# Turning the recurrence's gated output on VectorE and GpSimd, with two columns of the output projection interleaved

## The chip, the cores and the metric

The kernel runs on one core of a Trainium2 chip. The metric is the time of one execution in device microseconds (us), as the median of several runs. A core has a matrix engine (TensorE; PE in the profile, its weight loads PEld), VectorE (DVE), ScalarE (ACT), GpSimd (POOL) and SyncE (SP), which issues the weight loads from memory. The engines run their own instruction lists in order and meet at semaphores.

## What is computed

Two transformer-like blocks on one sequence of 256 rows of 2048 numbers: a gated convolution layer, a gated linear recurrence layer (HGRN2), sliding window attention, and a gated feed-forward layer. The change touches the end of the recurrence layer:

```python
def hgrn2_mixer(h, w_in, lb_fwd, lb_bwd, o_norm, w_out):
    u = h @ w_in
    q, a_f, a_b, i, z = jnp.split(u, 5, axis=-1)
    ...
    o = rms_norm(o_fwd + o_bwd, o_norm)
    o = o.transpose(0, 2, 1, 3).reshape(B, S, WIDTH).astype(h.dtype)
    return (o * jax.nn.silu(z)) @ w_out
```

`y = o * silu(z)` is 256 rows by 2048 channels, and the product `y @ w_out` needs it with channels on the partitions, so y must be transposed before the projection.

## The kernel before

Every weight matrix is streamed in chunks of 256 rows by 512 columns (512 KB). A chunk passes four engines: SP loads it into `raw` (four slots), ACT rounds it to `w_hi` (L906), DVE computes the rest `w_lo = raw - w_hi` (L1293), and PE does twelve matmuls with it (L644, L645, L646: high by high, low by high, high by low, for two halves of the contraction and two blocks of rows). ACT may round chunk n only when PE has used chunk n-4. All engines run the same loop over chunks (`stream`), and everything else is hung into this loop by hand: `Hooks().put(i, step)` runs a step on that engine right behind its work on chunk i. So the order of work on an engine is the order of the chunk numbers, and within one number the order of the `put` calls. A step hooked to chunk i of DVE comes before DVE's `w_lo` of chunk i+1, and an engine that waits in a step lets everything behind it wait too.

The stretch at issue is the phase `hgrn_z` (32 chunks, the product that gives z, four column groups of 512) and the phase `hgrn_out` behind it (32 chunks, the output projection, four columns of eight chunks each). Hooks count on from one phase to the next, so chunk 32 is the first of `hgrn_out`. The text numbers chunks this way, from 0 at the start of `hgrn_z` to 63 at the end of `hgrn_out`.

The output of the recurrence comes in four groups of 512 channels. For group k DVE multiplies (`gate(k)`, L1597, into `gate_rows[k]`, that is aftok, abtok, qtok, sz); PE transposes eight 128x128 blocks into the accumulator memory T (`gated_turn(k)`, L595); ACT rounds them to `y_hi` (`hz_hi(k)`, L1181); DVE computes `hy_lo` (`z_lo(k)`, L1298). `GATE_AT = [29, 31, 33, 35]` places PE's four transposes behind chunks 29, 31, 33 and 35; ACT's step is three chunks later and DVE's four (z_lo(0) at 32, z_lo(1) at 35, z_lo(2) at 37, z_lo(3) at 39). The projection takes group k in its chunks 2k and 2k+1 of each column, and PE waits in front of each chunk of the first column until the group is there (`need`, semaphore g_lo).

Group 3's last factor is late: DVE's `o_norm(3)` (L1546, L1548, hook 32) gives sums, GpSimd's `o_power(3)` (L516) raises them to -0.5, DVE's `o_scale(3)` (L1553, L1555, hook 34) waits for that and scales, and `gate(3)` follows at hook 35, behind z_lo(1). GpSimd has nothing else to do in this stretch.

The result of each column is added to x by DVE (`residual`, L1329), two chunks after the column's end. PE has two pairs of accumulators, used in turn by the columns, so column 2 can't begin before column 0's residual. From x, three of the four groups are transposed for the next layer by DVE in blocks of 32x32 (`x_turn`, L1346) and by GpSimd, which moves the blocks between the partition quarters with 16 copies (`x_moves`, L506); the same pair of steps serves the recurrence's inputs (L1581, L522).

Of the kernel before, what the change touches and what calls it, by code (L numbers as in the profile page):

```python
# [30 lines left out]
ACT = mybir.ActivationFunctionType  # L31
# [6 lines left out]
TB = S // P  # L38
# [23 lines left out]
FIRST_LOWS = 2 * CPG  # L62
ACT_TAKES = 4
HB = P // 2
GATE_AT = [29, 31, 33, 35]
TURNED_PARTS = [(2 * c, 2 * c + 2) for c in range(CPG)]
WARM = 14

# [11 lines left out]
class Phase:  # L80
# [6 lines left out]
    def __init__(self, iters, per_iter, chunk0, pair0, uses0, chunks=CPG, columns=4, turns=None):  # L87
        self.chunk0, self.pair0, self.uses0 = chunk0, pair0, uses0
        assert iters == 1 or per_iter % 2 == 0
        self.uses_per = [sum(self.pair(k) == p for k in range(per_iter)) for p in range(2)]  # L90
        self.seq = [(k, c) for k in range(per_iter) for c in range(chunks)]
        if per_iter == 2 * columns:
            self.seq = [(p * columns + k, c) for p in range(2) for ks, cs in (((0, 1), (0, 1)), ((0, 1), (2, 3)), ((2,), range(4)), ((3,), range(4)))
                        for k in ks for c in cs]
        self.seq0 = self.seq
        if turns:
            self.seq0 = [(k, c) for a, b in zip((0, *turns), turns) for k in range(2) for c in range(a, b)] + [kc for kc in self.seq if kc[0] > 1]
        self.last0 = {k: i for i, (k, c) in enumerate(self.seq0) if c == chunks - 1}
        self.last = {k: i for i, (k, c) in enumerate(self.seq) if c == chunks - 1}
        self.chunks, self.in_parts, self.columns = chunks, per_iter == 2 * columns, columns  # L100
        self.chunk1 = chunk0 + iters * len(self.seq)
        self.uses1 = [uses0[p] + iters * self.uses_per[p] for p in range(2)]
# [37 lines left out]
def phases():  # L140
    out, chunk, pair, uses = {}, 0, 0, [0, 0]
    for name, iters, per, more in (
            ("conv_ab", 4, 2, {}), ("conv_z", 1, 4, {}), ("conv_out", 1, 4, {}), ("hgrn", 4, 4, {"turns": (6, 8)}),
            ("hgrn_z", 1, 4, {}), ("hgrn_out", 1, 4, {}), ("kv_q", 1, 5, {}), ("att_out", 1, 8, {"chunks": CPG // 2}),
            ("gate_up", FJ, 2, {"turns": (4, 6, 8)}), ("down", 1, 4, {"chunks": FCH})):
        out[name] = Phase(iters, per, chunk, pair, uses, **more)
        pair = out[name].pair(iters * per)
        chunk, uses = out[name].chunk1, out[name].uses1
    return out
# [23 lines left out]
def build(nc, t, out):  # L173
    ph = phases()
    ctx = ExitStack()
    with ctx:
# [3 lines left out]
        def sem(name):  # L180
            return ctx.enter_context(nc.semaphore(name))
# [106 lines left out]
        def operands(s):  # L288

            b = (s - 1) % 4 if s else 1  # L290
            return (E_more if b >= 2 else E)[:, b % 2, :, :, :]

        def gate_banks(k):
            return T01 if k % 2 else T23

# [17 lines left out]
        g_raw, g_q, g_M, g_act, g_lb, g_D, g_E, g_G, g_mm, g_S = (  # L313
            sem(f"hgrn_{s}") for s in ("raw", "quarters", "moved", "act", "lb", "D", "E", "G", "mm", "S"))
        g_sb, g_K = sem("hgrn_blocks"), sem("hgrn_keys")
        g_av, g_o, g_ss, g_std, g_on, g_zr, g_z, g_y, g_yT, g_hi, g_lo = (
            sem(f"hgrn_{s}") for s in ("av", "o", "ss", "std", "on", "zr", "z", "y", "yT", "yhi", "ylo"))
        a_cs, a_ang, a_ev, a_sq, a_ss, a_std, a_rp, a_T, a_cp = (
# [25 lines left out]
        def by_channel(t):  # L344
            return t.rearrange("p a (b c) -> p (a b) c", c=S)

        x_quarters = (None, 2 * (atok[:, :, :],), 2 * (sm[:, 0:2, :],), (aq[:, :, :], kvtok))
        x_moved = (None, 2 * (by_channel(sq[:, :, :]),), 2 * (by_channel(sm[:, 2:4, :]),), (by_channel(ar), by_channel(asq)))

        def on_tensor(s):  # L350

# [1 line left out]

        def moved_buffers(s):

            return 2 if s == 3 else 1

        def groups_turned(s):

# [19 lines left out]
        def flat(ap):  # L379
            return ap.rearrange("p a b -> p (a b)")  # L380
# [97 lines left out]
        def _(pool):  # L478
# [34 lines left out]
            def o_power(j):  # L513
                nc.gpsimd.drain()
                pool.wait_ge(g_ss, j + 1)
                nc.gpsimd.tensor_tensor(ssh[:, 2, :], ssh[:, 1, :], powers[:, :], ALU.pow).then_inc(g_std, 1)  # L516
                nc.gpsimd.drain()

            def moves(dst, src, quarters):
                for a in quarters:  # L520
                    for b in range(4):
                        last = nc.gpsimd.tensor_copy(turned_block(dst, a, b), own_block(src, a, b))  # L522
                return last

            for j in range(4):
                pool.wait_ge(g_q, 3 * j + 1)
                moves(kf, sz, range(4)).then_inc(g_M, 1)
                pool.wait_ge(g_q, 3 * j + 2)
                moves(kb, aftok, range(2))
                if j:  # L530
                    o_power(j - 1)
                moves(kb, aftok, range(2, 4)).then_inc(g_M, 1)
                pool.wait_ge(g_q, 3 * j + 3)
                moves(qT, abtok, range(4)).then_inc(g_M, 1)
            o_power(3)

            x_moves(2)

# [50 lines left out]
        def _(pe):  # L589
# [207 lines left out]

            def gated_turn(k):
                pe.wait_ge(g_y, k + 1)
                if k < 2:  # L800
                    pe.wait_ge(*((g_o, 8) if k else (g_S, 36)))
                else:
                    pe.wait_ge(g_lo, 2 * (k - 1))
                transposes(gate_banks(k), gate_rows[k], g_yT)
            at = process(3)
            for k in range(4):
                at.put(GATE_AT[k], lambda k=k: gated_turn(k))
            stream("hgrn_z", 0, h_hi, h_lo, at)
            stream("hgrn_out", 0, y_hi, hy_lo, at.later(32),
# [77 lines left out]
        def _(act):  # L887
# [46 lines left out]
            def x_squares(s, k):  # L934
                if s == 0:
                    act.wait_ge(x_in[k], 16)
                else:
                    act.wait_ge(x_done, 4 * (s - 1) + k + 1)
                nc.scalar.drain()
                for tb in range(TB):  # L940
                    last = A(fg[:, tb, :], x[:, tb, group_columns(k)], ACT.Square, accum_out=ssq[:, tb, k:k + 1])
                last.then_inc(n_sq, 1)
# [5 lines left out]
            def x_norm(name, s):  # L948
                at = Hooks()
                for k in range(4):  # L950
                    e = ph[name].end(k)
                    at.put(e + 3, lambda k=k: x_squares(s, k)).put(e + {1: (8, 8, 8, 8), 2: (8, 8, 8, 4), 3: (6, 9, 9, 9)}[s][k], lambda k=k: x_hi(s, k))
                return at.put(ph[name].end(3) + 5, lambda: x_std(s))


# [202 lines left out]
            def rest(j):  # L1158
                return Hooks() if isinstance(j, int) and j < 0 else process(j).later(32)
# [18 lines left out]
            def hz_hi(k):  # L1178
                act.wait_ge(g_yT, k + 1)
                for b in range(2):  # L1180
                    A(flat(y_hi[:, 4 * k + 2 * b:4 * k + 2 * b + 2, :]), gate_banks(k)[:, b, :], ACT.Copy).then_inc(g_hi, 1)  # L1181
            at = Hooks().put(3, lambda: raw_out(3, 3, vtok)).with_(process(3)).with_(rest(2))
            for k in range(4):
                at.put(8 * k + 10, lambda k=k: hz_out(k)).put(GATE_AT[k] + 3, lambda k=k: hz_hi(k))
                if k < 3:
                    at.put(28 + k, lambda k=k: hz_silu(k))
            stream("hgrn_z", 0, at)
# [84 lines left out]
        def _(dve):  # L1272
# [84 lines left out]
            def x_norm(name, s):  # L1357
                at = Hooks()
                for k in range(4):
                    e = ph[name].end(k)  # L1360
                    at.put(e + 2, lambda k=k: residual(name, k)).put(e + {1: (9, 9, 9, 9), 2: (9, 9, 9, 5), 3: (7, 10, 10, 10)}[s][k], lambda k=k: x_lo(s, k))
                    if k < on_tensor(s):
                        at.put(e + 3, lambda k=k: x_turn(s, k))
                    if ph[name].in_parts:
                        at.put(ph[name].last[k] + 3, lambda k=k: first_part(name, k))
                return at.put(ph[name].end(3) + 4, lambda: x_sums(s)).put(ph[name].end(3) + 6, lambda: x_rstd(s))
# [232 lines left out]
            def z_lo(k):  # L1599
                for b in range(2):  # L1600
                    dve.wait_ge(g_hi, 2 * k + b + 1)
                    kk = slice(4 * k + 2 * b, 4 * k + 2 * b + 2)
                    low(flat(hy_lo[:, kk, :]), gate_banks(k)[:, b, :], flat(y_hi[:, kk, :]), g_lo)
            at = Hooks().put(32, lambda: z_lo(0)).with_(process(3, 1)).with_(rest(2))
            for k in range(4):
                at.put((29, 30, 31, 35)[k], lambda k=k: gate(k))
                if k:
                    at.put(GATE_AT[k] + 4, lambda k=k: z_lo(k))
            stream("hgrn_z", 0, at)

            def angles():
# [231 lines left out]
```

## Time and profile before

| what | value |
|---|---|
| median of 3 runs | 1894.44 us (1893.97 to 1895.26) |
| the profiled execution | 1895.02 us |
| its span, first to last instruction | 1893.2 us |
| TensorE matmuls, busy | 1888.0 us, 100% of the span |
| VectorE busy | 1294.8 us, 68% |
| ScalarE busy | 1058.5 us, 56% |
| GpSimd busy | 655.8 us, 35% |
| granted TensorE clock | 1.000 on the mean of the span |

1.8 us of the profiled time lie outside the span. Busy shares say which engine is worth looking at; what ends a wait, and how much room an engine has before another waits for it, is read from the timelines below. Times in them are us from the start of the span.

### The profile page before, as it was taken

To read this page: it belongs to the slowest core of one execution; us is meant where nothing else is said; L and a number is where in the kernel's file an instruction comes from. 1 tells how busy PE (TensorE), PEld (TensorE's weight loads), DVE (VectorE), ACT (ScalarE), POOL (GpSimd) and SP (SyncE) were. 2 spreads that over 40 slices of the span, in tenths; PEclk is the share of its full clock that TensorE was granted. 3 is DMA by queue.
4 is the path that set the end of the run, shared out by engine and by line. 5 is a ranking of instruction groups with operands and counts; after the bars stand their busy time and mean duration, and the time that the engine had idled before them with its cause. 6 is when DMAs were issued, how large, how long until landed. Compare 5 with 4: busy or idle time off the path is not lost.

```text
span 1893.2 us, 28787 instructions
## 1 busy us (share of the span) xinstructions
PE 1888.0 (100%) x10832; PEld 1556.6 (82%) x10832; DVE 1294.8 (68%) x1877; ACT 1058.5 (56%) x1402; POOL 655.8 (35%) x705
## 2 busy tenths in 40 slices
PE   9999999999999999999999999999999999999999
PEld 8888878888888888788888888888888888888887
DVE  5899967645888888887668877655555555544443
ACT  7444466546878697875465755544444444443432
POOL 1899852516051423302418646422222222210000
PEclk9999999999999999999999999999999999999999
DMA  9666656666555555555565455666666666655564
GB/s 327 193 190 187 178 170 197 192 196 181 168 175 170 153 183 168 167 163 184 189 190 148 154 178 172 209 196 190 188 198 192 196 189 194 193 194 194 192 195 159
DMA packets 183600, 352.64 MB, mean 186 GB/s; under 512 B 11840, under 2 KB 12352, under 8 KB 183488
## 3 DMA queue, kind: packets, MB, share of 16 engines
q1 hardware_dynamic: 183344, 351.12, 60.6%
q8 instruction: 72, 1.18, 0.3%
q14 instruction: 40, 0.33, 0.1%
q10 hardware_dynamic: 144, 0.01, 0.0%
HBM read 348.99 MB, written 2.10 MB: 185 GB/s over the span
## 4 chain that ended last, share of the span: by engine, by line
PE 94%; DVE 2%; POOL 2%; ACT 1%; issue 1%; POOLq 0%; DVEq 0%; ACTq 0%
PE acc L644 30%; PE acc L646 29%; PE acc L645 29%; PE T L759 1%; DVE w_lo L1293 1%; PE T L595 1%; POOL apad L506 1%; POOL kb L522 1%; PE acc L611 1%; POOL kf L522 0%; PE T L860 0%; PE T L750 0%; PE T L839 0%; POOLq L507 0%; PE T L769 0%
## 5 line engine op out<-in xcount | busy, mean ns | idle before, releaser
L1293 DVE TENSOR_TENSOR w_lo<-raw,w_hi 128x1024 fp32r<-128x1024 f32 x564 | 696.8, 1238 | 508.5 <-ACT w_hi L906 498.3
L906 ACT ACTIVATE w_hi<-raw 128x1024 fp32r<-128x1024 f32 x655 | 687.4, 1057 | 607.5 <-PE acc L646 583.4
L644 PE MATMUL acc<-w_hi,h_hi 128*128 128x512 f32 x1872 | 735.0, 393 | 0.6 <-DVE w_lo L1293 0.6
L646 PE MATMUL acc<-w_hi,h_lo 128*128 128x512 f32 x1872 | 728.8, 389 | 0.0
L645 PE MATMUL acc<-w_lo,h_hi 128*128 128x512 f32 x1872 | 728.7, 389 | 0.0
L644 PEld LDWEIGHTS acc<-w_hi,h_hi 128*128 128x128 f32 x1872 | 351.4, 188 | 79.2 <-issue 4.2
L646 PEld LDWEIGHTS acc<-w_hi,h_lo 128*128 128x128 f32 x1872 | 351.4, 188 | 73.9
L645 PEld LDWEIGHTS acc<-w_lo,h_hi 128*128 128x128 f32 x1872 | 351.6, 188 | 70.9
L584 POOL COPY fT<-fq 32x256 f32<-32x256 f32 x176 | 111.6, 634 | 360.4 <-DVE fq L1775 353.5
L493 POOL TENSOR_TENSOR w_lo<-raw,w_hi 128x1024 fp32r<-128x1024 f32 x80 | 190.4, 2405 | 67.9 <-ACT w_hi L906 67.7
L1384 DVE SCALAR_TENSOR_TENSOR T<-vpad,feat,T 128x256 f32<-128x256 f32 x464 | 182.6, 502 | 0.0
L644 PE MATMUL acc<-w_hi,y_hi 128*128 128x512 f32 x384 | 151.0, 393 | 0.0
L645 PE MATMUL acc<-w_lo,y_hi 128*128 128x512 f32 x384 | 149.5, 389 | 0.0
L644 PE MATMUL acc<-w_hi,f_hi 128*128 128x512 f32 x352 | 136.9, 389 | 0.0
L645 PE MATMUL acc<-w_lo,f_hi 128*128 128x512 f32 x352 | 136.9, 389 | 0.0
L646 PE MATMUL acc<-w_hi,f_lo 128*128 128x512 f32 x352 | 136.9, 389 | 0.0
L522 POOL COPY kf<-sz 32x256 f32<-32x256 f32 x64 | 37.3, 582 | 255.9 <-DVEq L1279 253.4
L646 PE MATMUL acc<-w_hi,hy_lo 128*128 128x512 f32 x256 | 99.7, 389 | 0.0
L644 PEld LDWEIGHTS acc<-w_hi,y_hi 128*128 128x128 f32 x384 | 72.1, 188 | 17.6 <-DVE y_lo L1298 1.6
L645 PEld LDWEIGHTS acc<-w_lo,y_hi 128*128 128x128 f32 x384 | 72.1, 188 | 14.5
L645 PEld LDWEIGHTS acc<-w_lo,f_hi 128*128 128x128 f32 x352 | 66.1, 188 | 13.8
L644 PEld LDWEIGHTS acc<-w_hi,f_hi 128*128 128x128 f32 x352 | 66.1, 188 | 13.7
(256 smaller groups left out, 1596.3 us busy)
## 6 DMA issues: line engine op xcount, KB each, us to landing
raw<-in_hgrn_w_in_dram SPq DMA_DIRECT2D x160, 512.0 KB, 3.6
raw<-in_conv_w_in_dram SPq DMA_DIRECT2D x96, 512.0 KB, 4.2
raw<-in_ffn_w_gate_dram SPq DMA_DIRECT2D x88, 512.0 KB, 4.4
raw<-in_ffn_w_up_dram SPq DMA_DIRECT2D x88, 512.0 KB, 4.2
raw<-in_ffn_w_down_dram SPq DMA_DIRECT2D x88, 512.0 KB, 4.6
raw<-in_attn_w_qkv_dram SPq DMA_DIRECT2D x40, 512.0 KB, 3.9
raw<-in_conv_w_out_dram SPq DMA_DIRECT2D x32, 512.0 KB, 4.3
raw<-in_hgrn_w_out_dram SPq DMA_DIRECT2D x32, 512.0 KB, 4.3
```

Of the source, the lines that this page charges most:

```text
L493: nc.gpsimd.tensor_tensor(w_lo[:, slot, :, :], raw[:, slot, :, :], rounded(w_hi[:, slot, :, :]), ALU.subtract).then_inc(split_ready, 1)
L506: nc.gpsimd.tensor_copy(turned_block(x_moved[s][k % 2], a, b), own_block(x_quarters[s][k % 2], a, b))
L522: last = nc.gpsimd.tensor_copy(turned_block(dst, a, b), own_block(src, a, b))
L584: last = nc.gpsimd.tensor_copy(turned_block(fT, a, b), own_block(fq, a, b))
L595: last = nc.tensor.transpose(dst[:, q // 2, at:at + P], src[:, tb, q * P:(q + 1) * P], ident[:, :])
L611: last = nc.tensor.matmul(acc[:, 0, tb, :], stationary[:, n * CK + kk, a], moving[:, n, kk, :], start=first and kk == 0, stop=False)
L644: nc.tensor.matmul(o, hi[:, kt, a], w_hi[:, slot, kk, :], start=c == 0 and kk == 0, stop=False)
L645: nc.tensor.matmul(o, hi[:, kt, a], w_lo[:, slot, kk, :], start=False, stop=False)
L646: last = nc.tensor.matmul(o, lo[:, kt, a], w_hi[:, slot, kk, :], start=False, stop=c == p.chunks - 1 and kk == CK - 1)
L906: A(w_hi[:, slot, :, :], raw[:, slot, :, :], ACT.Copy).then_inc(hi_ready, 1)
L1293: TT(w_lo[:, slot, :, :], raw[:, slot, :, :], rounded(w_hi[:, slot, :, :]), ALU.subtract).then_inc(split_ready, 1)
L1384: STT(out=cy[:, kt, :] if tap == TAPS - 1 else y, in0=v, scalar=w, in1=y, op0=ALU.mult, op1=ALU.add).then_inc(c_tap, 1)
```

## The change

Groups 0 and 1 are transposed by PE as before. Groups 2 and 3 are transposed by DVE in 32x32 blocks (`gate_turn`, two transposes each, into kf and kb) and moved between quarters by GpSimd (16 copies each, into Bc and Xc, which are free by then). ACT then rounds such a group in one instruction of 128x1024 (`hz_moved_hi`) and DVE computes its low part in one (`z_moved_lo`). GpSimd does the first eight copies of group 2 ahead of `o_power(3)` and the rest behind it.

`hgrn_out` gets `"turns": (4, 6, 8)`: its first two columns run as four chunks of column 0, four of column 1, then two and two, and two and two. So group 2 is first needed at chunk 40 in place of 36, group 3 at chunk 44 in place of 38. Column 0 ends after chunk 45 and column 1 after chunk 47 (before: 39 and 47). The steps that hang on a column's end move along: residual(0) from chunk 42 to 48, x_turn(0) from 43 to 49. SP loads the chunks in the new order. On DVE `gate(3)` now stands ahead of `z_lo(1)` at chunk 35, because of the order of the `put` calls. The transposes of x in this phase get a second pair of buffers.

```diff
-GATE_AT = [29, 31, 33, 35]
+GATE_AT = [29, 31]
...
+        if iters == 1:
+            self.seq = self.seq0
...
-            ("hgrn_z", 1, 4, {}), ("hgrn_out", 1, 4, {}), ("kv_q", 1, 5, {}), ("att_out", 1, 8, {"chunks": CPG // 2}),
+            ("hgrn_z", 1, 4, {}), ("hgrn_out", 1, 4, {"turns": (4, 6, 8)}), ("kv_q", 1, 5, {}), ("att_out", 1, 8, {"chunks": CPG // 2}),
...
-            return 2 if s == 3 else 1
+            return 2 if s > 1 else 1
...
+            pool.wait_ge(g_yq, 1)
+            moves(gate_moved[2], gate_quarters[2], range(2))
             o_power(3)
+            moves(gate_moved[2], gate_quarters[2], range(2, 4))
+            nc.gpsimd.drain().then_inc(g_yM, 1)
+            pool.wait_ge(g_yq, 2)
+            moves(gate_moved[3], gate_quarters[3], range(4))
+            nc.gpsimd.drain().then_inc(g_yM, 1)
...
             def gated_turn(k):
                 pe.wait_ge(g_y, k + 1)
-                if k < 2:
-                    pe.wait_ge(*((g_o, 8) if k else (g_S, 36)))
-                else:
-                    pe.wait_ge(g_lo, 2 * (k - 1))
+                pe.wait_ge(*((g_o, 8) if k else (g_S, 36)))
                 transposes(gate_banks(k), gate_rows[k], g_yT)
             at = process(3)
-            for k in range(4):
+            for k in range(2):
                 at.put(GATE_AT[k], lambda k=k: gated_turn(k))
...
-                    at.put(e + 3, lambda k=k: x_squares(s, k)).put(e + {1: (8, 8, 8, 8), 2: (8, 8, 8, 4), 3: (6, 9, 9, 9)}[s][k], lambda k=k: x_hi(s, k))
+                    at.put(e + 3, lambda k=k: x_squares(s, k)).put(e + {1: (8, 8, 8, 8), 2: (8, 11, 8, 4), 3: (6, 9, 9, 9)}[s][k], lambda k=k: x_hi(s, k))
...
+            def hz_moved_hi(k):
+                act.wait_ge(g_yM, k - 1)
+                A(flat(y_hi[:, 4 * k:4 * k + 4, :]), flat(gate_moved[k][:, :, :]), ACT.Copy).then_inc(g_hi, 2)
...
+            at.put(38, lambda: hz_moved_hi(2)).put(42, lambda: hz_moved_hi(3))
...
-                    at.put(e + 2, lambda k=k: residual(name, k)).put(e + {1: (9, 9, 9, 9), 2: (9, 9, 9, 5), 3: (7, 10, 10, 10)}[s][k], lambda k=k: x_lo(s, k))
+                    at.put(e + 2, lambda k=k: residual(name, k)).put(e + {1: (9, 9, 9, 9), 2: (9, 12, 9, 5), 3: (7, 10, 10, 10)}[s][k], lambda k=k: x_lo(s, k))
...
+            def gate_turn(k):
+                settle()
+                for tb in range(TB):
+                    last = V.transpose(gate_quarters[k][:, tb, :], gate_rows[k][:, tb, :])
+                last.then_inc(g_yq, 1)
+
+            def z_moved_lo(k):
+                dve.wait_ge(g_hi, 2 * k + 2)
+                kk = slice(4 * k, 4 * k + 4)
+                TT(flat(hy_lo[:, kk, :]), flat(gate_moved[k][:, :, :]), rounded(flat(y_hi[:, kk, :])), ALU.subtract).then_inc(g_lo, 2)
             at = Hooks().put(32, lambda: z_lo(0)).with_(process(3, 1)).with_(rest(2))
             for k in range(4):
                 at.put((29, 30, 31, 35)[k], lambda k=k: gate(k))
-                if k:
-                    at.put(GATE_AT[k] + 4, lambda k=k: z_lo(k))
+            at.put(31, lambda: gate_turn(2)).put(GATE_AT[1] + 4, lambda: z_lo(1)).put(36, lambda: gate_turn(3))
+            at.put(39, lambda: z_moved_lo(2)).put(43, lambda: z_moved_lo(3))
             stream("hgrn_z", 0, at)
```

## Rows read from the trace of the kernel before

**Rows 1.** The page: busy times, and the granted clock in 40 slices.
```profile
PE 1888.0 (100%) x10832; PEld 1556.6 (82%) x10832; DVE 1294.8 (68%) x1877; ACT 1058.5 (56%) x1402; POOL 655.8 (35%) x705
...
PEclk9999999999999999999999999999999999999999
```

**Rows 2.** The waits of PE: waiter, awaited: us in total, times, longest.
```profile
PE acc L644 <- DVE w_lo L1293: 0.6, 2, 0.4
```

**Rows 3.** Timeline of PE, 862 to 864: start, duration, engine, line, operation.
```profile
862.42 0.39 PE L646 MATMUL acc<-w_hi,hy_lo 128*128 128x512 f32 x1
...
863.44 0.48 PE L644 MATMUL acc<-w_hi,y_hi 128*128 128x512 f32 x1
...
863.99 0.39 PE L646 MATMUL acc<-w_hi,hy_lo 128*128 128x512 f32 x1
```

**Rows 4.** The line of PE's transposes: duration min/median/max in ns, first and last start.
```profile
L595 PE MATMUL T<-ident,qtok x8: 270/273/273, 862.6 to 863.4; 128*128 128x128 f32 x8
```

**Rows 5.** Timeline of DVE, 849 to 864 (brackets: idle ahead, its releaser).
```profile
849.65 1.22 DVE L1597 TENSOR_TENSOR qtok<-qtok,o_all 128x1024 f32<-128x1024 f32 x1
...
852.04 1.28 DVE L1298 TENSOR_TENSOR hy_lo<-T,y_hi 128x512 fp32r<-128x512 f32 x2
...
854.60 2.36 DVE L1293 TENSOR_TENSOR w_lo<-raw,w_hi 128x1024 fp32r<-128x1024 f32 x2
857.35 1.22 DVE L1553 TENSOR_TENSOR E<-E,ssh 128x1024 f32<-128x1024 f32 x1 [0.39 <-POOL ssh L516]
...
860.86 1.23 DVE L1293 TENSOR_TENSOR w_lo<-raw,w_hi 128x1024 fp32r<-128x1024 f32 x1 [0.99 <-ACT w_hi L906]
862.00 1.28 DVE L1298 TENSOR_TENSOR hy_lo<-T,y_hi 128x512 fp32r<-128x512 f32 x2
863.20 1.22 DVE L1597 TENSOR_TENSOR sz<-sz,o_all 128x1024 f32<-128x1024 f32 x1
```

**Rows 6.** Timeline of DVE, other places: a scale, a transpose pair, residuals.
```profile
755.85 1.23 DVE L1553 TENSOR_TENSOR E<-E,ssh 128x1024 f32<-128x1024 f32 x1 [2.08 <-POOL ssh L516]
...
758.33 1.41 DVE L1293 TENSOR_TENSOR w_lo<-raw,w_hi 128x1024 fp32r<-128x1024 f32 x1
...
883.55 1.30 DVE L1346 STREAM_TRANSPOSE sm<-x 128x512 f32<-128x512 f32 x2
884.86 1.23 DVE L1293 TENSOR_TENSOR w_lo<-raw,w_hi 128x1024 fp32r<-128x1024 f32 x1
...
899.80 2.56 DVE L1293 TENSOR_TENSOR w_lo<-raw,w_hi 128x1024 fp32r<-128x1024 f32 x2
...
905.00 1.28 DVE L1329 TENSOR_TENSOR x<-acc,x 128x512 f32<-128x512 f32 x2
...
908.08 1.22 DVE L1293 TENSOR_TENSOR w_lo<-raw,w_hi 128x1024 fp32r<-128x1024 f32 x1
```

**Rows 7.** Timeline of POOL: runs of copies in short windows, and two powers (L516).
```profile
440.81 0.39 POOL L522 COPY kf<-sz 32x256 f32<-32x256 f32 x1 [56.67 <-DVEq L1279]
...
738.87 4.34 POOL L522 COPY kf<-sz 32x256 f32<-32x256 f32 x8 [64.48 <-DVEq L1279]
...
754.18 1.64 POOL L516 TENSOR_TENSOR ssh<-ssh,powers 128x8 f32<-128x8 f32 x1
...
755.96 1.36 POOL L522 COPY kb<-aftok 32x256 f32<-32x256 f32 x1
...
854.77 2.54 POOL L516 TENSOR_TENSOR ssh<-ssh,powers 128x8 f32<-128x8 f32 x1 [80.39 <-DVE ssh L1548]
...
910.58 7.05 POOL L506 COPY sm<-sm 32x256 f32<-32x256 f32 x8 [14.76 <-DVE sm L1346]
```

**Rows 8.** Timeline of PE: the first matmuls of chunks 48 and 51.
```profile
902.54 0.39 PE L644 MATMUL acc<-w_hi,y_hi 128*128 128x512 f32 x1
...
910.70 0.39 PE L644 MATMUL acc<-w_hi,y_hi 128*128 128x512 f32 x1
```

**Rows 9.** Groups by line, 836 to 946: count | busy, mean | idle before.
```profile
L906 ACT ACTIVATE w_hi<-raw 128x1024 fp32r<-128x1024 f32 x38 | 39.4, 1054 | 22.3 <-PE acc L646 22.1 <-issue 0.2
```

More of the change, by code:

```diff
@@ L291, in operands @@
             return (E_more if b >= 2 else E)[:, b % 2, :, :, :]
+        gate_quarters = (None, None) + tuple(t[:, :, :].rearrange("p a b -> p (a b)").rearrange("p (a b) -> p a b", a=TB) for t in (kf, kb))
+        gate_moved = (None, None, Bc, Xc)
         def gate_banks(k):
@@ L315, in build @@
         g_sb, g_K = sem("hgrn_blocks"), sem("hgrn_keys")
+        g_yq, g_yM = sem("hgrn_yquarters"), sem("hgrn_ymoved")
         g_av, g_o, g_ss, g_std, g_on, g_zr, g_z, g_y, g_yT, g_hi, g_lo = (
@@ L345, in by_channel @@
             return t.rearrange("p a (b c) -> p (a b) c", c=S)
-        x_quarters = (None, 2 * (atok[:, :, :],), 2 * (sm[:, 0:2, :],), (aq[:, :, :], kvtok))
-        x_moved = (None, 2 * (by_channel(sq[:, :, :]),), 2 * (by_channel(sm[:, 2:4, :]),), (by_channel(ar), by_channel(asq)))
+        x_quarters = (None, 2 * (atok[:, :, :],), (sm[:, 0:2, :], sm[:, 4:6, :]), (aq[:, :, :], kvtok))
+        x_moved = (None, 2 * (by_channel(sq[:, :, :]),), (by_channel(sm[:, 2:4, :]), by_channel(sm[:, 6:8, :])), (by_channel(ar), by_channel(asq)))
         def on_tensor(s):
@@ L1181, in hz_hi @@
                     A(flat(y_hi[:, 4 * k + 2 * b:4 * k + 2 * b + 2, :]), gate_banks(k)[:, b, :], ACT.Copy).then_inc(g_hi, 1)
+            def hz_moved_hi(k):
+                act.wait_ge(g_yM, k - 1)
+                A(flat(y_hi[:, 4 * k:4 * k + 4, :]), flat(gate_moved[k][:, :, :]), ACT.Copy).then_inc(g_hi, 2)
             at = Hooks().put(3, lambda: raw_out(3, 3, vtok)).with_(process(3)).with_(rest(2))
+            at.put(38, lambda: hz_moved_hi(2)).put(42, lambda: hz_moved_hi(3))
             for k in range(4):
-                at.put(8 * k + 10, lambda k=k: hz_out(k)).put(GATE_AT[k] + 3, lambda k=k: hz_hi(k))
+                at.put(8 * k + 10, lambda k=k: hz_out(k))
+                if k < 2:
+                    at.put(GATE_AT[k] + 3, lambda k=k: hz_hi(k))
                 if k < 3:
```

## The prediction

> **What bounds the kernel now.** The page comes first: PE is busy for 1888.0 us of a span of 1893.2, no other engine for over 68%, and PE's clock is granted in full (2.4 GHz) in all 40 slices [rows 1]. The list of PE's waits comes second, since a busy PE may still stand: it waited for work of the stream 0.6 us in all [rows 2]. So PE's own instructions set the end. What leaves PE is gained, what makes PE wait is lost, one for one, and nothing later gives it back. The question is then whether each engine still brings its result before PE asks for it, which is read from the timelines of PE, DVE and POOL around the edit. All clock times below are those of the trace of before. A chunk takes PE 2.72 us: from the first matmul of chunk 48 to that of chunk 51 it is 8.16 us [rows 8].
>
> **What leaves PE.** Two of four groups of eight transposes. Between the two matmuls around such a group, at 862.42 and 863.99, lie three steps of the stream, which take 3 x 0.227 = 0.68 us elsewhere; so a group costs 1.57 - 0.68 = 0.89 us of PE [rows 3]. Two groups: -1.8 us. I take this, and not the durations, as transposes overlap: eight of 273 ns would be 2.2 us a group [rows 4].
> The Trainium skill, TensorE: Matmul & The Clock Gate, Part 4 (PE-mode transpose), gives about 275 ns for a 128x128 transpose in a kernel; the trace has the same duration, but a gain summed from it, 4.4 us for sixteen, would be over twice what the spacing allows.
>
> **What is late in its place.** PE enters chunk 34 when group 1's low part is there: that is z_lo(1). In the trace z_lo(1) runs from 862.00 to 863.28 [rows 5] and PE starts chunk 34 at 863.44 [rows 3]. PE had finished chunk 33 at about 862.6 and spent the time until then on the transposes of group 2. These covered z_lo(1); they go, so even with DVE unchanged PE would wait about 0.7 us. And DVE doesn't stay unchanged. Step by step:
> - gate(2) starts at 849.65 and takes 1.22 [rows 5]. The new transposes of group 2 follow behind a drain: start 850.9. A pair takes 1.30, and the next instruction comes 1.31 after its start [rows 6]. So they end at 852.2, and z_lo(0) (was 852.04) and the two w_lo (were at 854.60) move by 1.35; these two end at 858.3. Chunk 33, which PE starts at 859.8, has its w_lo long before. This shift costs PE nothing.
> - GpSimd starts the first eight copies at 852.3. It must finish them before o_power(3), whose sums are ready at 854.77 + 1.35 = 856.1. What do eight copies cost? The trace has 4.34 us and 7.05 us as ends [rows 7]. The copies themselves differ: 0.39 us when alone, 1.36 us when a DVE tensor_tensor with both inputs in the large memory runs at the time (the copy at 755.96 beside L1553 at 755.85) [rows 6, 7]. Here w_lo(32) starts as the first copy does, w_lo(33) and w_lo(34) lie over the seventh and eighth: 3 x 1.36 + 5 x 0.43 = 6.2 us, end 858.5.
> - The power took 2.54 us beside two w_lo, and 1.64 us with DVE waiting [rows 7]. Here DVE waits. With 0.15 for the drain and 0.04 to DVE: o_scale(3) starts at 858.5 + 0.15 + 1.64 + 0.04 = 860.3. It started at 857.35 [rows 5], so +2.95. From both sides: 4.34 + 1.64 gives 858.4 (+1.1), 7.05 + 2.54 gives 862.0 (+4.7). I take the middle value, since three held copies follow from the order of DVE's instructions.
> - Behind the scale stands w_lo(35), 2.48 us after its start as at 755.85 and 758.33 [rows 6]. In the trace DVE idled 0.99 us ahead of it for ACT's w_hi(35), ready at 860.8 [rows 5]; that idle time is used up. Then comes gate(3), now ahead of z_lo(1): 1.2 us. So z_lo(1) ends at 863.28 + 2.95 - 0.99 + 1.2 = 866.4 (ends: 864.6 and 868.2).
> PE starts chunk 34 at 866.45 in place of 863.44: +3.0 (ends +1.2, +4.8). It stands idle from 862.8, about 3.6 us. This sum already holds the gain of group 2's transposes. Group 3's add -0.9. Net **+2.1 us** (ends +0.3, +3.9).
>
> The Trainium skill, GPSIMD Engine Reference, Key points, says that GpSimd shares its interfaces to SBUF with VectorE and contends with instructions that have two SBUF inputs. It speaks against this change. By that rule the trace agrees as far as the copies and the power go (1.36 against 0.39 us); DVE's side shows no price, w_lo takes 1.23 us beside copies at 884.86.
>
> **Edits that should cost nothing, and their cover.**
> - Groups 2 and 3 themselves. In the new kernel chunk 40 starts at 866.45 + 6 x 2.72 = 882.8, chunk 44 at 893.7. Eight more copies, all held, 11 us, end by 871.6; ACT can round w_hi(39) once PE has left chunk 35, at 871.9; three instructions of about 1.2 us behind it give group 2 at 875.6, 7 us early. Group 3: sixteen copies take twice the 4.34 or 7.05 us of eight [rows 7], so they end by 871.6 + 14.1 = 885.7; w_hi(42) or its like, the rounding, w_lo(43) and the low part (4 x 1.2) give 890.5, 3 us early.
> - ACT: two instructions of 1.06 us take the place of four shorter ones; in this stretch it idles 22.1 us waiting for PE [rows 9]. No idle time there is put down to a weight load, so SP's new order of the same 32 loads costs nothing either.
> - Column 2 (chunk 48) needs residual(0), now behind angles (hook 47) and w_lo(48). DVE starts w_lo(48) at 899.80, PE starts chunk 48 at 902.54 [rows 6, 8]. Residual after w_lo: 899.80 + 1.15 + 1.28 = 902.2. It arrives 0.3 us early. Then w_lo(49) at 902.4, x_turn(0) (1.31), w_lo(50) at 904.9, residual(1) and the rotations, which held DVE from 905.00 to 908.08 [rows 6]: w_lo(51) from 909.1 to 910.3, PE wants it at 910.70. It is 0.4 us early. Both gaps are thin, and they don't add up, since lateness is counted once: 0 taken, 0 to +1 as bounds. In before, residual(0) lay eight chunks earlier in a calm place.
> - POOL's moves for x start 20 us later; with two buffers x_turn(1) and x_turn(2) no longer wait for one another, and ACT's steps were moved along. 0.
>
> **The rivals.**
> 1. PE's clock falls (slower). A PE idle for 3.6 us is nothing that this trace shows: the longest wait for the stream is 0.4 us and the clock is at its upper level throughout [rows 1, 2]. If the idle time makes the clock drop to 1.2 GHz, PE does each following chunk in 5.4 us rather than 2.72 while that lasts. Twelve matmuls at half pace add 2.7 us, two chunks 5.4: 1894.44 + 2.1 + 2.7 = 1899.2, or 1901.9. It decides from the length of the idle stretch, so it goes with the upper end of the copies' cost. The Trainium skill, TensorE: Matmul & The Clock Gate (What's actually happening), says that the clock falls to the lower level after an idle stretch; no row here shows from where on.
> 2. DVE is on time (gain in full). If the copies and the power hide under DVE's own work, or z_lo(1) does not stand behind them as I read the hooks, PE loses only its transposes: 1894.44 - 1.8 = 1892.6. Against it: the low ends of all rows together still give +0.3, and o_scale(3) already waited 0.39 us for the power without the copies [rows 5].
> 3. The hand-over of columns slips too: PE waits at chunk 48 or 51. +1 on the forecast: 1897.5. For it: margins of 0.3 and 0.4 us; against: they rest on the same chain of instructions as in before.
>
> **How the numbers follow.** The sum is made on the profiled execution, 1895.02 us, of which 1.8 lie outside its span; +2.1 gives 1897.1 for it. It is 0.6 above the median of 1894.44, so the forecast for the median is 1894.44 + 2.1 = **1896.5 us**. Chances: forecast 0.66, rival 1 0.12, rival 2 0.1, rival 3 0.12. The range takes in the forecast's ends (1894.7 to 1898.3), rivals 2 and 3 and the short form of rival 1: 1892.6 to 1899.2. About 0.2% (3.8 us) is what a measurement of this kernel can tell from no change. Slower by over that, above 1898.2, are rival 1 and the far end of forecast with rival 3: 0.16. Faster, below 1890.7, is in no case; 0.02 for what I don't see. Within it: 0.82.
>
> **What would show it.** In the profile after: PE's list of waits has a new entry at chunk 34, for DVE's hy_lo (L1298's line), of 2 to 5 us; POOL's eight copies take 6.2 us from about 852.3; DVE's wait for the power ahead of o_scale(3) grows from 0.4 to about 2; DVE runs gate(3) right ahead of the second z_lo. If PE's waits stay below 1 us in all, rival 2 holds; a granted clock below 1.00 in a slice near the middle is rival 1; a wait of PE for the residual's line or w_lo near chunk 48 is rival 3. A time under 1893.5 would refute the sum: then the order of DVE's work is not as I read it.

## The result

| kernel | median us (lowest to highest) | executions | profiled execution, its span |
|---|---|---|---|
| before | 1895.29 (1893.97 to 1896.08) | 10 | 1895.02, 1893.2 |
| changed | 1900.57 (1898.66 to 1901.79) | 10 | 1901.14, 1899.3 |

The changed kernel is slower: the ratio is 1.0029, with a 95% interval of 1.0021 to 1.0036. That is +5.3 us, above the range of the prediction (1892.6 to 1899.2) and in the direction that it forecast.

The waits of PE come first. They have one new row, which stands against [rows 2]: PE waited once, for 4.2 us, for the low part `hy_lo` that z_lo(1) writes (L1315 here, L1298 before; L657 to L659 are L644 to L646 before).

```profile
PE acc L657 <- DVE hy_lo L1315: 4.2, 1, 4.2
...
PE acc L657 <- DVE w_lo L1310: 0.6, 2, 0.4
```

The timeline of PE around that wait answers to [rows 3]. PE ends chunk 33 and starts chunk 34. This execution is 0.79 us late against that of before at the end of chunk 33 (863.21 against 862.42), which arose well ahead of the edit: PE's opening matmuls already start 0.6 us later. I take these 0.79 us off in what follows.

```profile
863.21 0.39 PE L659 MATMUL acc<-w_hi,hy_lo 128*128 128x512 f32 x1
867.82 0.80 PE L657 MATMUL acc<-w_hi,y_hi 128*128 128x512 f32 x1 [4.22 <-DVE hy_lo L1315]
868.41 0.63 PE L658 MATMUL acc<-w_lo,y_hi 128*128 128x512 f32 x1
868.84 0.63 PE L659 MATMUL acc<-w_hi,hy_lo 128*128 128x512 f32 x1
...
873.53 0.50 PE L658 MATMUL acc<-w_lo,y_hi 128*128 128x512 f32 x1
873.87 0.39 PE L659 MATMUL acc<-w_hi,hy_lo 128*128 128x512 f32 x1
874.10 0.40 PE L657 MATMUL acc<-w_hi,y_hi 128*128 128x512 f32 x1
```

Two things are to be seen. Chunk 34 starts at 867.82 - 0.79 = 867.03, where it started at 863.44: +3.6 us. And then the matmuls start 0.427 us apart, not 0.227, until 873.53. The table by stretch of time says why; its columns are the stretch, its length, busy time and count for PE, PEld, DVE, ACT and POOL, the granted clock of PE, and the DMA share and rate.

```profile
866.00:867.00 1.00, 0.00 (x0) 0.00 (x0) 1.00 (x2) 0.00 (x0) 0.96 (x2) 0.96 0.49 160
867.00:873.00 6.00, 5.18 (x12) 4.12 (x13) 4.30 (x6) 0.00 (x0) 4.96 (x8) 0.50 0.51 162
873.00:874.00 1.00, 1.00 (x4) 0.77 (x4) 0.00 (x0) 0.60 (x1) 0.91 (x3) 0.63 0.92 303
```

The granted clock fell to half, 1.2 GHz, near 866.9, when PE had stood idle for over three of its four microseconds, and rose again near 873.7, with PE at work since 867.8. From 867.82 to 873.87 PE makes 14 steps in 6.05 us, where 14 x 0.227 = 3.18; of the 2.87 us more, 0.08 belong to the first step, which was as long in before (863.44 to 863.75 in its trace). So the half pace costs 2.8 us. The page's line of 40 slices can't show it: each slice is 47 us, and all digits are 9, as in [rows 1].

The account: +3.6 for the late start, +2.8 for the half pace, -0.9 for group 3's transposes, which PE no longer does: +5.5. By the traces chunk 48 starts at 908.82 - 0.79 = 908.03 in place of 902.54 [rows 8], +5.5; by the medians +5.3. What comes behind adds nothing beyond 0.2 us.

VectorE's timeline from 851 to 868 answers to [rows 5], with the copies and the power of GpSimd below it, which answer to [rows 7].

```profile
851.83 1.30 DVE L1625 STREAM_TRANSPOSE kf<-qtok 128x512 f32<-128x512 f32 x2
853.05 1.18 DVE L1310 TENSOR_TENSOR w_lo<-raw,w_hi 128x1024 fp32r<-128x1024 f32 x1
...
856.72 2.55 DVE L1310 TENSOR_TENSOR w_lo<-raw,w_hi 128x1024 fp32r<-128x1024 f32 x2
861.34 1.22 DVE L1570 TENSOR_TENSOR E<-E,ssh 128x1024 f32<-128x1024 f32 x1 [2.07 <-POOL ssh L522]
862.64 1.26 DVE L1572 TENSOR_TENSOR o_all<-E,onorm 128x1024 f32<-128x1024 f32 x1
863.82 1.41 DVE L1310 TENSOR_TENSOR w_lo<-raw,w_hi 128x1024 fp32r<-128x1024 f32 x1
865.16 1.41 DVE L1614 TENSOR_TENSOR sz<-sz,o_all 128x1024 f32<-128x1024 f32 x1
866.49 1.27 DVE L1315 TENSOR_TENSOR hy_lo<-T,y_hi 128x512 fp32r<-128x512 f32 x2
```

```profile
853.19 6.34 POOL L528 COPY Bc<-kf 32x256 f32<-32x256 f32 x8 [77.97 <-DVE kf L1625]
859.67 1.64 POOL L522 TENSOR_TENSOR ssh<-ssh,powers 128x8 f32<-128x8 f32 x1
861.45 8.14 POOL L528 COPY Bc<-kf 32x256 f32<-32x256 f32 x8
870.36 11.44 POOL L528 COPY Xc<-kb 32x256 f32<-32x256 f32 x16 [0.76 <-DVE kb L1625]
```

This is the chain that the prediction wrote down: two transposes, eight copies, the power, the scale, w_lo(35), gate(3), z_lo(1), and PE at its end. VectorE stands 2.07 us for the power, where it stood 0.39. That the chain is the cause, and the idle time the cause of the clock's fall, is so far read from one trace. The experiments test it.

### The profile page after: what moved, and what is told of

It reads as the page before. It is cut to its first block, busy times and chain, and to the rows that moved or that the text cites. A ratio compares the mean times of both kernels' runs of the same rounds, so it can differ in the third digit from the quotient of the medians.

```text
span 1899.3 us, 28792 instructions
## 1 busy us (share of the span) xinstructions
PE 1889.9 (100%) x10816; PEld 1557.3 (82%) x10816; DVE 1300.9 (68%) x1879; ACT 1058.8 (56%) x1400; POOL 681.8 (36%) x737
## 3 DMA queue, kind: packets, MB, share of 16 engines
q8 instruction: 72, 1.18, 0.3%
## 4 chain that ended last, share of the span: by engine, by line
PE 91%; DVE 4%; POOL 2%; ACT 1%; issue 1%; POOLq 1%; DVEq 0%; ACTq 0%
PE acc L657 29%; PE acc L659 29%; PE acc L658 29%; DVE w_lo L1310 1%; PE T L772 1%; POOL apad L512 1%; POOL kb L528 1%; PE T L608 1%; PE acc L624 1%; POOL kf L528 0%; PE T L870 0%; ACT w_hi L916 0%; DVEq L1296 0%; PE T L763 0%; PE T L849 0%
## 5 line engine op out<-in xcount | busy, mean ns | idle before, releaser
L657 PE MATMUL acc<-w_hi,h_hi 128*128 128x512 f32 x1872 | 735.1, 393 | 0.6 <-DVE w_lo L1310 0.6
L659 PE MATMUL acc<-w_hi,h_lo 128*128 128x512 f32 x1872 | 728.8, 389 | 0.0
L657 PEld LDWEIGHTS acc<-w_hi,h_hi 128*128 128x128 f32 x1872 | 351.4, 188 | 79.8 <-issue 4.2
L659 PEld LDWEIGHTS acc<-w_hi,h_lo 128*128 128x128 f32 x1872 | 351.4, 188 | 73.6
L657 PE MATMUL acc<-w_hi,y_hi 128*128 128x512 f32 x384 | 152.1, 396 | 4.2 <-DVE hy_lo L1315 4.2
L657 PE MATMUL acc<-w_hi,f_hi 128*128 128x512 f32 x352 | 136.9, 389 | 0.0
L659 PE MATMUL acc<-w_hi,f_lo 128*128 128x512 f32 x352 | 136.9, 389 | 0.0
L659 PE MATMUL acc<-w_hi,hy_lo 128*128 128x512 f32 x256 | 100.6, 393 | 0.0
L657 PEld LDWEIGHTS acc<-w_hi,y_hi 128*128 128x128 f32 x384 | 72.7, 189 | 22.1 <-DVE hy_lo L1315 4.6
L659 PEld LDWEIGHTS acc<-w_hi,f_lo 128*128 128x128 f32 x352 | 66.1, 188 | 13.8
```

The costliest lines, as they stand in the source:

```text
L657: nc.tensor.matmul(o, hi[:, kt, a], w_hi[:, slot, kk, :], start=c == 0 and kk == 0, stop=False)
L659: last = nc.tensor.matmul(o, lo[:, kt, a], w_hi[:, slot, kk, :], start=False, stop=c == p.chunks - 1 and kk == CK - 1)
```

## The experiments

Each kernel was timed beside the kernel before on the same chip, whose median there was 1895.29 to 1895.52 us. The runs were spread over several chips (e1, e2, e4 and e5 on one, e3, e6 and e7 on another, e8 on a third), so the difference of two medians from different chips is less sure than a ratio; where a trace settles a size, it is named. Theory A is the prediction's chain plus rival 1: the low part of group 1 is late, and PE's clock falls because PE stands idle. Theory B puts the loss into the interleaved columns or GpSimd's copies, with the clock falling of itself. All diffs are against the changed kernel unless said.

| run | what differs | median us | ratio to before (95%) | PE's wait for hy_lo, us | executions with a mean clock below 1.000 |
|---|---|---|---|---|---|
| changed | | 1900.57 | 1.0029 (1.0021 to 1.0036) | 4.2 | 10 of 10 |
| e8 | second copies later | 1899.82 | 1.0022 (1.0013 to 1.0031) | 3.8 | 11 of 11 |
| e2 | z_lo(1) ahead of gate(3) | 1898.40 | 1.0015 (1.0006 to 1.0024) | 2.7 | 10 of 11 |
| e1 | power first | 1896.39 | 1.0008 (0.9999 to 1.0017) | 2.2 | 4 of 11 |
| e5 | idle time filled | 1898.12 | 1.0013 (1.0004 to 1.0022) | 1.5 | 0 of 11 |
| e3 | e1 and e2 | 1894.71 | 0.9995 (0.9986 to 1.0004) | 0.9 | 0 of 11 |
| e4 | z_lo(1) ahead of the scale | 1893.62 | 0.9992 (0.9983 to 1.0001) | none | 0 of 11 |
| e7 | e4 and 16 transposes on PE | 1895.30 | 0.9999 (0.9990 to 1.0008) | none | 0 of 11 |
| e6 | before and the interleaving | 1895.48 | 1.0001 (0.9992 to 1.0010) | none | 0 of 11 |

**The order on GpSimd (e1).**

```diff
+            o_power(3)
             pool.wait_ge(g_yq, 1)
-            moves(gate_moved[2], gate_quarters[2], range(2))
-            o_power(3)
-            moves(gate_moved[2], gate_quarters[2], range(2, 4))
+            moves(gate_moved[2], gate_quarters[2], range(4))
```

> The changed kernel with o_power(3) ahead of all copies of group 2 on GpSimd. Theory A (late low part, then a falling clock): the power starts when its sums are there, so o_scale(3) moves by 1.4 us against the kernel before instead of 3.2; PE's wait for z_lo(1) is about 2.2 us instead of 4.2, and the clock stays at its upper level: time 0.5 to 0.8 above the kernel before, about 1896.0 us, 4.5 below the changed kernel. Theory B (the loss comes from the interleaved columns or from GpSimd's copies beside VectorE, and the clock falls of itself): the time stays within 1 us of the changed kernel's, 1900.6.

Measured 1896.39 us; in the profiled execution PE waited 2.25 us:

```profile
865.34 0.50 PE L656 MATMUL acc<-w_hi,y_hi 128*128 128x512 f32 x1 [2.25 <-DVE hy_lo L1314]
```

So the eight copies ahead of the power, and not the interleaving, are half of the wait. But the clock did not stay up each time, as I had expected. Seven executions, with a clock of 1.000, took 1895.83 to 1896.49 us; four, with a clock of 0.999, took 1897.99 to 1898.46. With the same instructions the two sets are 2.0 us apart. I take this as the price of a fall; that these four executions had the same wait as the others is not shown, since only one execution, with the clock up, was profiled.

**The order on VectorE (e2).**

```diff
+            at.put(GATE_AT[1] + 4, lambda: z_lo(1))
             for k in range(4):
                 at.put((29, 30, 31, 35)[k], lambda k=k: gate(k))
-            at.put(31, lambda: gate_turn(2)).put(GATE_AT[1] + 4, lambda: z_lo(1)).put(36, lambda: gate_turn(3))
+            at.put(31, lambda: gate_turn(2)).put(36, lambda: gate_turn(3))
```

> The changed kernel with z_lo(1) ahead of gate(3) at chunk 35, one instruction of VectorE swapped. Theory A: PE's wait shrinks by 1.3 us to 2.9. If that is too short for the clock to fall, the time is 1.4 above the kernel before, 1896.7 us; if the clock falls all the same, 1899.3. Theory B: no change to the changed kernel beyond the 1.3 us.

One instruction swapped, 2.2 us less. The wait is 2.7 us, 1.5 less, as expected within 0.2, and the time lies between the two values that I gave, since the clock falls but for a shorter time. In the profiled execution it was low only from about 866.3 to 869.7:

```profile
866.00:867.00 1.00, 0.55 (x1) 0.63 0.55 168
867.00:869.00 2.00, 2.00 (x6) 0.50 0.51 178
869.00:870.00 1.00, 1.00 (x4) 0.67 0.16 14
```

(PE alone: stretch, length, busy time and count, clock, DMA share and rate.) The low stretch is half as long as in the changed kernel, and the half pace costs 1.5 us here, by the same reckoning, and not 2.8.

**Both orders (e3).** The two diffs above together.

> The changed kernel with both orders mended: o_power(3) ahead of all copies, z_lo(1) ahead of gate(3), but z_lo(1) still behind o_scale(3). Theory A: PE still waits 0.9 us for z_lo(1) (2.25 less 1.3 of the run with the power first), the clock never falls, in no run: 0.5 us below the kernel before, 1894.9 us.

Measured 1894.71 us, a wait of 0.9 us, and a mean clock of 1.000 in all 11 executions. (To three digits a mean of 1.000 could hide a low stretch of under 2 us, here and in e5; in the profiled execution of each there is none around chunk 34.) The interval of the ratio still takes in 1.

**No wait at all (e4).**

```diff
-            at = Hooks().put(32, lambda: z_lo(0)).with_(process(3, 1)).with_(rest(2))
+            at = Hooks().put(32, lambda: z_lo(0)).put(34, lambda: z_lo(1)).with_(process(3, 1)).with_(rest(2))
...
-            at.put(31, lambda: gate_turn(2)).put(GATE_AT[1] + 4, lambda: z_lo(1)).put(36, lambda: gate_turn(3))
+            at.put(31, lambda: gate_turn(2)).put(36, lambda: gate_turn(3))
```

> The changed kernel with z_lo(1) hooked to chunk 34, ahead of o_scale(3), so that nothing behind the power stands between PE and group 1. Theory A: no wait of PE, full clock, only the gain of two groups of transposes is left: 1.8 us below the kernel before, 1893.5 us. Theory B (columns): still near 1899 to 1900.

Measured 1893.62 us, 7 us below the changed kernel, with the copies, the turned groups and the interleaved columns all still in place. VectorE does z_lo(1) in the time in which it would have stood waiting for the power:

```profile
858.51 1.28 DVE L1315 TENSOR_TENSOR hy_lo<-T,y_hi 128x512 fp32r<-128x512 f32 x2
860.66 1.23 DVE L1570 TENSOR_TENSOR E<-E,ssh 128x1024 f32<-128x1024 f32 x1 [0.88 <-POOL ssh L522]
```

The power still comes late, and it no longer matters. This refutes theory B: nothing but the place of one step was moved. Against the kernel before e4 has the lower median by 1.8 us, the whole gain that the change could give; its highest execution (1894.48) lies just above the lowest of 33 of the kernel before (1894.33), and the ratio's interval ends at 1.0001, so "faster than before" is probable and not shown beyond doubt.

**What PE's transposes cost (e7).** e4, with this on PE, called behind chunks 33 and 35:

```diff
+            def filler(n):
+                pe.wait_ge(g_lo, 2)
+                for _ in range(n):
+                    for q in range(4):
+                        for tb in range(TB):
+                            c = (q % 2) * S + tb * P
+                            nc.tensor.transpose(T23[:, q // 2, c:c + P], aftok[:, tb, q * P:(q + 1) * P], ident[:, :])
+            at.put(33, lambda: filler(1))
+            at.put(35, lambda: filler(1))
```

> The kernel with z_lo(1) ahead of o_scale(3) (run e4), with two groups of eight transposes put back on PE behind chunks 33 and 35, whose results nobody reads. It measures the price of what the change takes from PE. By the spacing in the trace, 0.89 us a group: 1.8 us above e4, 1895.4 us, as the kernel before. By the durations of the transposes, 2.2 us a group: 4.4 above e4, 1898.0.

Measured 1895.30, 1.7 us above e4: 0.84 us a group. Two medians from two chips don't fix this to a tenth, but e7's own trace does. Around its first group:

```profile
863.05 0.39 PE L659 MATMUL acc<-w_hi,hy_lo 128*128 128x512 f32 x1
863.28 1.03 PE L825 MATMUL T<-ident,aftok 128*128 128x128 f32 x8
...
864.62 0.39 PE L659 MATMUL acc<-w_hi,hy_lo 128*128 128x512 f32 x1
```

The two matmuls are 1.57 us apart, as in before, and so they are around the second group (869.38 to 870.95): 0.89 us each. The spacing was the right price, the sum of durations (2.2) was not.

**Idle time and clock (e5).** The changed kernel with `at.put(33, lambda: filler(3))`: 24 transposes inside the wait.

> The changed kernel with 24 transposes on PE behind chunk 33 whose results nobody reads; they lie inside PE's wait of 4.2 us and take some 2.6 of it. Theory A: chunk 34 starts as late as in the changed kernel, but PE's clock stays up, so the 2.7 us of half pace are gone: 1897.9 us. If the clock falls whatever PE does there, 1900.6.

Measured 1898.12 us. Chunk 34 starts as late as in the changed kernel (4.5 us after the start of chunk 33's last matmul, where it was 4.6), and behind it the matmuls start at full pace:

```profile
863.42 2.78 PE L825 MATMUL T<-ident,aftok 128*128 128x128 f32 x24
867.68 0.50 PE L657 MATMUL acc<-w_hi,y_hi 128*128 128x512 f32 x1 [1.49 <-DVE hy_lo L1324]
868.02 0.40 PE L658 MATMUL acc<-w_lo,y_hi 128*128 128x512 f32 x1
```

Work that nobody uses made the kernel 2.4 us faster, and the mean clock was 1.000 in all 11 executions. So the fall is caused by PE's idleness, and the two parts of the loss, lateness and half pace, are told apart.

**The interleaving alone (e6).** The kernel before with `"turns": (4, 6, 8)`, the moved x steps and the second pair of buffers, and no transposes moved.

> The kernel before with the interleaved first two columns of the output projection, the later steps that go with them (residual, squares, x_hi, x_lo) and the second pair of buffers for x, but with all four groups transposed on PE as before. Theory A: the interleaving costs nothing by itself, PE has no wait near chunks 48 and 51: within 0.5 us of the kernel before, 1895.4 us. If residual(0) behind the angles makes PE wait at chunk 48, PE's list of waits shows it and the time is about 1 us higher.

Measured 1895.48 against 1895.39: nothing. PE has no wait for the stream above 0.4 us.

**GpSimd's copies beside VectorE (e8).** The prediction had w_lo(35) and gate(3) at 1.22 us; in the changed kernel each took 1.41.

```diff
             o_power(3)
+            pool.wait_ge(g_yq, 2)
             moves(gate_moved[2], gate_quarters[2], range(2, 4))
```

> The changed kernel, in which GpSimd's second eight copies of group 2 wait until group 3 is turned, so that no copy runs beside VectorE's w_lo(35) and gate(3). These two took 1.41 us each in the changed kernel with copies beside them, where 1.22 was forecast. If the copies slow VectorE, both go back to 1.22, PE's wait shrinks from 4.2 to 3.8 us and the time falls by 0.4 to about 1900.2 us (more if the clock's low stretch gets shorter). If not, they stay at 1.41 and the wait stays at 4.2.

Both went back to 1.22 us, and PE's wait to 3.8:

```profile
863.20 1.22 DVE L1311 TENSOR_TENSOR w_lo<-raw,w_hi 128x1024 fp32r<-128x1024 f32 x1
864.34 1.22 DVE L1615 TENSOR_TENSOR sz<-sz,o_all 128x1024 f32<-128x1024 f32 x1
```

```profile
869.35 4.36 POOL L528 COPY Bc<-kf 32x256 f32<-32x256 f32 x8 [8.63 <-DVE kb L1626]
```

The same eight copies took 8.14 us beside VectorE and 4.36 us here. So the two slow each other, and the copies pay most. The median is 0.75 lower, of which 0.4 is the wait; the intervals of the two ratios overlap, so the price of the copies rests on the two traces and not on the medians.

## Why the prediction was wrong, point by point

- **What bounds the kernel, and what leaves PE: right.** 0.89 us a group was forecast; e7 measured 0.84 by the medians and 0.89 in its trace. The sum of durations would have been 2.5 times too large.
- **The chain behind z_lo(1): right, step by step.** Eight copies 6.2 us (6.34), with the first, seventh and eighth held as forecast (1.30, 1.47 and 1.30 us), the power 1.64 (1.64), the scale's start 860.3 (861.34 - 0.79 = 860.55), gate(3) ahead of z_lo(1), PE's new wait at chunk 34. e1, e2 and e4 each took away a link, and the wait fell by 2.0, 1.5 and all of it.
- **The size of that term: +3.0 forecast, +3.6 measured.** 0.25 of the difference is the scale's start. The rest is mainly w_lo(35) and gate(3), 1.41 us each where 1.22 was taken: the prediction said that VectorE's side shows no price for copies beside it, resting on w_lo at 884.86. That was read from one row too few. The w_lo at 758.33 in [rows 6] took 1.41 us with copies beside it, and stood in the prediction's own rows. e8 shows the price.
- **The step that failed: the clock.** The sum priced PE's 3.6 us of idle time at its own length and left the clock at its upper level; the fall stood beside it as rival 1, at a chance of 0.12. In the changed kernel the mean clock was below 1.000 in all ten executions, and in the profiled one the half pace cost 2.8 us, the largest part of the miss. The forecast's own 3.6 us of idle time would have been enough: with profiled waits of 2.7 (e2) and 3.8 us (e8) the clock fell in 21 of 22 executions, so the fall did not need the upper end of the copies' cost, as rival 1 had it. The rival's price for one chunk, 2.7 us, came out right by luck: no row said that the low pace would last one chunk and not two. The prediction said that no row shows how the clock reacts to such a wait; that was so, and it was a reason to give the rival half of the chances and the range its longer form, not an eighth.
- **The base.** The forecast stands on 1894.44 us, the median of three executions; the ten beside the changed kernel gave 1895.29. This is 0.85 of the miss of 4.1 us (1900.57 against 1896.5) and has nothing to do with the change. With 0.6 for the lateness and 2.8 for the clock the terms come to 4.2. On the forecast's base, both true sizes give 1894.44 + 2.7 + 2.8 = 1899.9, still above the range's end of 1899.2, which was rival 1 with the forecast's lateness.
- **Rival 2 (on time)** was rightly set aside as the kernel stands; e4 shows that it was one hook away. **Rival 3 (columns)** did not come. Forecast were margins of 0.3 and 0.4 us; measured were 0.9 and 0.4, in the changed kernel and in e6 alike. For the changed kernel these are residual(0) against chunk 48 and w_lo(51) against chunk 51:

```profile
906.66 1.28 DVE L1346 TENSOR_TENSOR x<-acc,x 128x512 f32<-128x512 f32 x2
908.82 0.39 PE L657 MATMUL acc<-w_hi,y_hi 128*128 128x512 f32 x1
...
915.19 1.36 DVE L1310 TENSOR_TENSOR w_lo<-raw,w_hi 128x1024 fp32r<-128x1024 f32 x1
916.98 0.39 PE L657 MATMUL acc<-w_hi,y_hi 128*128 128x512 f32 x1
```

- **Groups 2 and 3** came early enough, as forecast: in no run does PE wait for them.

By the Trainium skill, TensorE: Matmul & The Clock Gate (What's actually happening), the clock falls after idleness; e5 against the changed kernel agrees, with 2.4 us between them. Its GPSIMD Engine Reference (Key points) names the contention of GpSimd with VectorE instructions that have two SBUF inputs; e8 agrees, in both directions.

## What to carry to other kernels

Work that is taken from the bounding engine may have been covering a wait: before removing it, look up what else that engine was about to wait for, and move that step forward in its engine's list (here z_lo(1), one hook, 7 us). A wait of TensorE can cost twice, once as time and once as clock: here waits of 2.7 us and more did so in 31 of 32 executions. Where such a wait can't be removed, it is worth trying to fill it with unused work, as 24 transposes did in e5. Price small instructions of TensorE by how far they push their neighbours apart, not by their durations.

## What was not expected of the hardware

- The mean clock was below 1.000 after short waits: in 4 of 11 executions at a wait of 2.2 us, 10 of 11 at 2.7, all 11 at 3.8 and all 10 at 4.2, and in none of 11 at 0.9 or at 1.5 (there behind 24 transposes). The waits are those of one profiled execution of each kernel. So the same kernel does it in one execution and not in the next; whether the wait itself differed between them is not known.
- A fall cost 2.0 us in e1 by the times, 2.8 us in the changed kernel's trace and 1.5 in e2's; the low stretch lasted about 6.8 us in the changed kernel's trace and 3.4 in e2's. Why it differs stays open.
- Beside GpSimd's copies a VectorE instruction with two inputs in the large memory can take 1.41 us, not 1.22, and eight copies 8.14 us, not 4.36. Not every such instruction pays: w_lo at 853.05, under which the first copy starts 0.14 us later, took 1.18.
